# Mixer to output projection: sums, statistic, loads and units in another order around the last pairs

## What is computed

```python
uv = gelu(h @ w_in); u, v = split(uv, 2)            # w_in: 1024 x 4096
v = rmsnorm(v, v_norm_g)                            # over its 2048 channels
z = einsum("gts,bnsgc->bntgc", tril(w_s), v) + b_s  # within chunks of 128 tokens, 8 groups
x = x + g1 * ((u * z) @ w_out)                      # g1 is a modulation vector of c
```

## Time and profile before

| | |
|---|---|
| runs | 2631.08, 2641.82, 2637.97 us; median 2637.97 |
| the profiled execution | 2636.03 us, span 2634.0 us |
| granted TensorE clock, mean over the span | 0.987 of full speed |
| busy share of the span | TensorE 96%, DVE 60%, ACT 37%, POOL 6% |
| HBM traffic | 270.10 MB read, 88.08 MB written |

### The profile page before, as it was taken

One profiled execution on the slowest core, in us unless ns is written; L12 is line 12 of the kernel. 1 busy time (PEld: TensorE's weight loads), 2 busy tenths in 40 slices (PEclk: granted clock), 3 DMA queues, 4 the chain that ended last, 5 costly groups with the idle time before them and its releaser, 6 DMA issues.

```text
span 2634.0 us, 33661 instructions
## 1 busy us (share of the span) xinstructions
PE 2536.5 (96%) x12220; PEld 2069.6 (79%) x12220; DVE 1583.4 (60%) x1907; ACT 985.4 (37%) x1423; POOL 149.7 (6%) x151
## 2 busy tenths in 40 slices
PE   6999979999999999999999997999999999999999
PEld 4787767888788878888898886666688888888887
DVE  6777746667876756666632543777347656544442
ACT  4543333234544431111311232777426544421110
POOL 0000000000000000000000001666100000000000
PEclk9999989999999999999999998999999999999999
DMA  6244544322344475554132353465313332632311
GB/s 252 100 152 153 179 176 156 117 100 112 110 161 148 149 294 199 179 204 154 52 136 82 112 156 121 107 142 113 128 62 126 111 117 100 254 133 80 111 49 71
DMA packets 122981, 359.60 MB, mean 137 GB/s; under 512 B 12033, under 2 KB 28417, under 8 KB 118913
## 3 DMA queue, kind: packets, MB, share of 16 engines
q1 hardware_dynamic: 122880, 358.23, 40.5%
HBM read 270.10 MB, written 88.08 MB: 136 GB/s over the span
## 4 chain that ended last, share of the span: by engine, by line
PE 80%; DVE 9%; ACT 4%; DMA 3%; issue 3%; SPq 0%; DVEq 0%; ACTq 0%
PE PS L2024 23%; PE PS L2026 23%; PE PS L2025 22%; DVE KEEP L1944 2%; PE PS L2500 2%; PE PS L2487 2%; DMA MODRAW<-in_modw 1%; PE PS L2468 1%; PE PS L2128 1%; PE PS L2130 1%; PE PS L2129 1%; ACT PS L1262 1%; PE PS L2424 1%; PE PS L2469 1%; DMA RAW<-in_wt 1%
## 5 line engine op out<-in xcount | busy, mean ns | idle before, releaser
L2024 PE MATMUL PS<-HID_HI,W_HI 128*128 128x512 f32 x1024 | 400.3, 391 | 5.1 <-DVE HID_LO L1597 4.9
L2025 PE MATMUL PS<-HID_LO,W_HI 128*128 128x512 f32 x1024 | 398.8, 389 | 0.0
L2026 PE MATMUL PS<-HID_HI,W_LO 128*128 128x512 f32 x1024 | 398.8, 389 | 0.0
L374 ACT ACTIVATE W_HI<-RAW 128x1024 fp32r<-128x1024 f32 x114 | 119.5, 1059 | 614.1 <-PE PS L2026 509.8
L1443 DVE SCALAR_TENSOR_TENSOR X<-PS,MODV,X 128x1024 f32<-128x1024 f32 x124 | 159.1, 1283 | 300.4 <-PE PS L2026 291.7
L2024 PE MATMUL PS<-H_HI,W_HI 128*128 128x512 f32 x700 | 277.7, 397 | 3.9 <-DVE H_LO L1387 2.7
L2026 PE MATMUL PS<-H_HI,W_LO 128*128 128x512 f32 x700 | 273.8, 391 | 0.0
L2025 PE MATMUL PS<-H_LO,W_HI 128*128 128x512 f32 x700 | 273.5, 391 | 0.0
L2024 PEld LDWEIGHTS PS<-HID_HI,W_HI 128*128 128x128 f32 x1024 | 192.3, 188 | 48.6 <-DVE HID_LO L1597 7.9
L2026 PEld LDWEIGHTS PS<-HID_HI,W_LO 128*128 128x128 f32 x1024 | 192.3, 188 | 40.2
L2025 PEld LDWEIGHTS PS<-HID_LO,W_HI 128*128 128x128 f32 x1024 | 192.3, 188 | 39.6 <-issue 0.2
(11 more groups left out here) (223 smaller groups left out, 4947.5 us busy)
## 6 DMA issues: line engine op xcount, KB each, us to landing
RAW<-in_wt SPq DMA_DIRECT2D x208, 512.0 KB, 4.1
MODRAW<-in_modw SPq DMA_DIRECT2D x96, 512.0 KB, 3.4
HRAW<-hid_scratch SPq DMA_DIRECT2D x14, 2048.0 KB, 8.9
hid_scratch<-TN SPq DMA_DIRECT2D x90, 256.0 KB, 2.7
hid_scratch<-SCR SPq DMA_DIRECT2D x84, 256.0 KB, 3.2
x_scratch<-X SPq DMA_DIRECT2D x3, 4096.0 KB, 13.8
X<-x_scratch SPq DMA_DIRECT2D x6, 2048.0 KB, 8.4
QK<-qk_scratch SPq DMA_DIRECT2D x16, 768.0 KB, 6.3
```

Source lines behind the costliest of these rows:

```text
L374: act.activation(ring_view(W_HI, n), raw_view(n), ACT.Copy).then_inc(sem["w_hi"], 1)
L2024: pe.matmul(dst, w_hi, m_hi, start=first, stop=False)
L2025: pe.matmul(dst, w_hi, m_lo, start=False, stop=False)
L2026: return pe.matmul(dst, w_lo, m_hi, start=False, stop=last)
```

## The change

- **Late modulation rows.** In pairs 6 to 11 the third `mod_reduce` goes behind `c12` and `c21`.
- **The second pair of each stage.** `c11` of pair 1 goes ahead of the cuts and sums for pair 2 on DVE (mixer and both MLPs).
- **The statistic.** The column sums with their waits go from ahead of pair 12 to behind its product 2, the spread from behind product 2 to behind product 5, and `v_inverse` behind three cuts.
- **Loads.** SP fetches units 0 and 1 of v once product 6 of pair 12 is done, and WS_RAW after product 7; the wait on `v_kept` is gone. In pair 13 loads of v and u stand ahead of X, and two stores ahead of the second half of X.
- **Units.** ACT and DVE cut the third and fourth weight tiles of the projection behind the first two units. `v_scale(1)` and `v_scale(2)` trade places with `v_lo(0)` and others.
- **Gates.** `spatial(2)` goes into gate 0, `turn_z(2)` behind it, and `turn_v(3)` into gate 1.

```diff
 # SP
-                u_pair(Count(PAIRS - 2), 0)
-                p = Count(PAIRS - 1)
-                sp.wait_ge(sem["product"], PRODUCTS * (PAIRS - 1))
+                p = Count(PAIRS - 2)
+                store(p, 0, 0, 0, 0)
+                load_pair(p + 1)
+                sp.wait_ge(sem["product"], count_of(0, p, PRODUCTS, 6).v)
...
                 load_v(0)
-                sp.wait_ge(sem["v_kept"], 1)
+                load_v(1)
+                store(p, 2, 0, 1, 1)
+                sp.wait_ge(sem["product"], count_of(0, p, PRODUCTS, 7).v)
                 sp.dma_start(WS_RAW[:], spw).then_inc(sem["spw_in"], 16)
-                load_v(1)
+                store(p, 3, 1, 2, 0)
+                store(p, None, 1, 3, 1)
+
+                p = Count(PAIRS - 1)
                 sp.wait_ge(sem["product"], count_of(0, p, PRODUCTS, 2).v)
                 load_u(0)
+                sp.wait_ge(sem["hs_out0"], 64 * (PAIRS // 2))
+                load_v(2)
                 load_u(1)
                 load_raw(sp, Count(T_G + 2))
+                load_v(3)
+                store(p, 0, 0, 0, 0)
                 sp.dma_start(X[:, 0:4, :], xT[:, 0:4, :]).then_inc(sem["xm_lo"], 16)
-                store(p, 0, 0, 0, 0)
-                sp.wait_ge(sem["hs_out0"], 64 * (PAIRS // 2))
-                load_v(2)
-                load_v(3)
                 load_raw(sp, Count(T_G + 3))
                 store(p, 2, 0, 1, 1)
                 sp.wait_ge(sem["product"], count_of(0, p, PRODUCTS, 6).v)
                 load_u(2)
                 load_u(3)
+                store(p, 3, 1, 2, 0)
+                store(p, None, 1, 3, 1)
...
                 sp.dma_start(X[:, 4:8, :], xT[:, 4:8, :]).then_inc(sem["xm_hi"], 16)
-                store(p, 3, 1, 2, 0)
-                store(p, None, 1, 3, 1)
 # ACT, pair 13
                 finish(p, 1, 6, 1)
-                act.wait_ge(sem["product"], count_of(0, p, PRODUCTS, 6).v)
-                down_cut(UPS + 2)
                 z_keep(1)
                 finish(p, 1, 7, 2)
-                act.wait_ge(sem["product"], count_of(0, p, PRODUCTS, 7).v)
-                down_cut(UPS + 3)
                 v_hi(2)
                 uz_cut(1)
+                act.wait_ge(sem["product"], count_of(0, p, PRODUCTS, 7).v)
+                down_cut(UPS + 2)
+                down_cut(UPS + 3)
 # DVE, pair
+                    second = p.i is None and p.c == 1
+                    if second:
+                        c11(p, x)
                     block_cut(p + 1, 1 - x, A1)
                     weight_sums(p + 1, 1 - x)
...
-                    c11(p, x)
-                    if kind == "stat":
-                        v_inverse()
+                    if not second:
+                        c11(p, x)
...
                     block_cut(p + 1, 1 - x, S3)
+                    if kind == "stat":
+                        v_inverse()
                     c22(p, x)
...
-                    elif kind in ("u0", "u"):
-                        mod_reduce(dve, p * 3 - 2 * VPAIRS + 2)
                     c12(p, x)
                     c21(p, x)
+                    if kind in ("u0", "u"):
+                        mod_reduce(dve, p * 3 - 2 * VPAIRS + 2)
 # DVE, pair 13
                 v_scale(0)
                 cut_lo(dve, Count(T_G))
-                v_scale(1)
...
                 v_lo(0)
+                v_scale(1)
                 cut_lo(dve, Count(T_G + 1))
+                v_scale(2)
...
                 v_lo(1)
-                v_scale(2)
-                cut_lo(dve, Count(T_G + 2))
                 c21(p, 1)
                 uz_mul(1)
-                cut_lo(dve, Count(T_G + 3))
                 v_lo(2)
                 uz_cut(1)
+                cut_lo(dve, Count(T_G + 2))
+                cut_lo(dve, Count(T_G + 3))
 # TensorE
-                for v in range(4 * KT):
+                gate(0, lambda: spatial(2))
+                turn_z(2)
+                gate(1, lambda: turn_v(3))
+                for v in range(2, 4 * KT):
...
                 def statistic(n):
                     if n == 2:
+                        pe.wait_ge(sem["v_added"], 6 + 4 * VPAIRS)
+                        pe.wait_ge(sem["mod_red"], GMODS)
+                        # the 8 column sums, from V_TOT to V_COLS
...
+                    if n == 5:
                         pe.wait_ge(sem["v_diag"], 2)
...
-                pe.wait_ge(sem["v_added"], 6 + 4 * VPAIRS)
-                pe.wait_ge(sem["mod_red"], GMODS)
-                # the 8 column sums
                 pair(Count(PAIRS - 2), 0, False, statistic)
```

More of the change, by code:

```diff
@@ L2375, in statistic @@
                     if n == 2:
+                        pe.wait_ge(sem["v_added"], 6 + 4 * VPAIRS)
+                        pe.wait_ge(sem["mod_red"], GMODS)
+                        for half in range(2):
+                            for c in range(4):
+                                mm = pe.matmul(V_COLS[:, 4 * half + c:4 * half + c + 1],
+                                               V_TOT[:, half, c * P:(c + 1) * P], ONES[:, 0:1], start=True, stop=True)
+                        mm.then_inc(sem["v_col"], 1)
+                    if n == 5:
                         pe.wait_ge(sem["v_diag"], 2)
```

## The result

The changed kernel took 2610.07 us, median of four runs (2604.66 to 2611.83), against 2636.21 for the kernel before in runs on the same chip: ratio 0.9904, 95% interval 0.9892 to 0.9916. The profiled execution took 2611.83 us, with a span of 2609.8 at clock 0.99, 24.2 us less than that of before. The forecast was 2599 in a range of 2592 to 2612. So the sign and the range hold. The time is 11 us above the forecast, and the medians of the two kernels differ by 26.1 us, where 39.0 were forecast. The time is that of rival 1.

What follows compares the result with a forecast made beforehand. TensorE, busy 96% of the span, was taken as the bound, so only its waits and half-clock time could be won. Gains of 6.6 + 3.9 + 28.5 = 39.0 us gave 2599 us, range 2592 to 2612.

Steps and rivals of the forecast that it cites:

- rival 1: Waits move into pair 13, mask chain late: stretch to `spatial(3)` gives 19, rest 9; 2610 us, chance 0.25.
- late rows: Mixer pairs 7 to 11: `c21` no longer behind the third reduction, product 2 stops waiting; 6.6 us, bounds 4 and 6.6.
- pair 1, mixer: `c11` moves into DVE's idle time, product 6 stops waiting, pair 2's wait grows; net gain 1.4 us.
- pair 1, MLP 0: The wait ahead of product 6 and its slow stretch go, 3.55 us; about 1.0 comes back in pair 2; net 2.5.
- pair 12 to `spatial(3)`: 93.9 us before, 62.9 of bare work plus 2.5 of waits after; gain 28.5 us, bounds 19 and 31.0.
- comes at 4.5 to 5 us: Pairs 7 to 11: when the A1 cut comes after pair start, RAW being asked for at about that start.
- take the same bytes: SP's moved loads and stores around pairs 12 and 13 were costed at nothing.
- Rival 2: Pair 12's statistic keeps its wait, the whole old 5.6 us, with rival 1 too: 20 us gained, 2618, chance 0.03.
- The order of the DVE chain after spatial 0: DVE, about 24 us nearly unbroken until `v_lo(2)`, meets the spatials and turns with waits of at most 0.3 us.
- the column sums without idle time: In pair 12 TensorE reaches them at 8.2 us, reductions done; 4.6 us wait gone, sums take 1.8 us.
- the bare work of 62.9 us: Pair 12 to `spatial(3)` at full clock without waits: two pairs, two gates, sums, spread, three spatials, seven turns.
- The clock: Slower rival: transposes among matmuls keep the clock low from pair 12 on; 2655 us, chance 0.02.

Runs made afterwards that it cites:

- again: The changed kernel run once more unaltered: 2610.30 us, 0.9909 of the kernel before.
- hold_stores: Changed kernel, but in mixer pairs 6 to 11 SP holds the last three stores, and the third modulation row's load, until ACT's A1 cut: 2601.44 us, 0.9867.
- hold_mask: Changed kernel with those stores held and, in pair 12, loads ordered RAW tile, v unit 0, WS_RAW, other tile, v unit 1: 2595.93 us, 0.9855.
- loads_undone: Changed kernel with SP's order of loads and stores around pairs 12 and 13 as before: 2610.61 us, 0.9912.

## Why the prediction came out as it did

**The total was off by 11 us, the sign and range right.** That the time fell inside the range is in part luck: the range reached up to 2612 only to take in rival 1, and two terms of the forecast's own mechanism were missed. By terms, in the two profiles of the changed kernel:

| us gained | forecast | after | again |
|---|---|---|---|
| late rows | 6.6 | 2.2 | 4.2 |
| pair 1, mixer | 1.4 | 0.0 | 1.8 |
| pair 1, MLP 0 | 2.5 | 1.9 | 2.8 |
| pair 12 to `spatial(3)` | 28.5 | 19.0 | 19.0 |

**The step that failed** is one clause in the part on late rows: that A1 "comes at 4.5 to 5 us". I had RAW asked for at the start of the pair and landing as fast as a modulation row, 3.5 us. In the trace of before A1 already came 8.8 us into pair 9 on DVE; with held stores it comes at 7.9 to 8.7 in pairs 7 to 11, which the room still covers. In the changed kernel it came at 8.7, 10.3, 12.0 and 13.9 us in pairs 7 to 10. ACT's cut came 6.4 us after the issue where I followed it, because the edit itself brings the stores forward, and each late cut makes the next issue later. The next sentence even had the mechanism: "each microsecond would first eat 4 us of room ahead of product 2". The chain falls behind TensorE by about 1.7 to 2.5 us per pair, so the room is gone after two or three pairs. Then it also makes the diagonals of pair 12 late, which I had put at 13.5 to 15.4 us against TensorE's arrival at 18.1. Pair 12 took 27.1 and 25.2 us in the two profiles against 22.7 with held stores, so this costs 4.5 and 2.5 us there. `hold_stores` gives all of it back.

**The second failed step** is that SP's moved loads "take the same bytes" and cost nothing. Bytes are the same, but WS_RAW stands behind 1 MB of RAW, two units of v and a store, all issued within 3.1 us. Its landing took 9.2 us (10.0 in the second profile) and not the 6.9 of the earlier trace rows that I used as the upper end. I took 1.3 us of wait at spatial 0; it was 3.6 (4.0), with a lower clock behind it.

**Two sums don't add up.** The waits that I named behind pair 12 are 1.3 and twice 0.3 us, 1.9 and not 2.5; no row is behind the other 0.6. And the least gains of the terms (4, 2 and 19) give 2613, not the 2606 that I named as the upper end of my own range.

**Rival 1** gave the very number, 2610, with 19 us for the stretch. A part of the match is luck: it took 28 us off 2638, where 26.1 were gained on 2636.2, and its other terms were to give 9 us, where the two profiles show 4.1 and 8.8. Half of its mechanism is right: the mask's chain is late, and brings half clock. But of the 9.5 us missing in the stretch 5.0 lay in pair 12 in the first profile and 3.1 in the second, around the spread, which neither the forecast nor rival 1 had; and of rival 1's second wait behind spatial 0 only 0.3 us was seen. Rival 2, the statistic's wait, came true in small: 2.2 us of 5.6, not by ACT's tables alone but by late weights, behind whose cuts the root stands, as held stores alone take it away.

**What held.** The order of the DVE chain after spatial 0 (no wait on DVE in gates 0 to 2), the column sums without idle time, the bare work of 62.9 us to within 1 us (`hold_mask` takes 64.7 with 0.8 us of waits, so 63.9), and the price of the late rows, once free of the stores. Also the small size of pair 1: the net of 1.4 us, the wait moving on to pair 2, is what most profiles show. In the first profile of the changed kernel that moved wait was 1.79 us and a stretch at clock 0.66 followed it, which ate the gain:

```profile
135.10 0.50 PE L2033 MATMUL PS<-T_HI,WX_HI 128*128 128x512 f32 x1 [1.79 <-DVE TN L1583]
```

```profile
135.00:140.00 5.00, 4.90 (x14) 3.88 (x15) 1.83 (x4) 3.15 (x5) 0.00 (x0) 0.66 0.92 344
```

**The clock.** In `hold_mask` seven turns lie within 64.7 us among the matmuls, and the granted clock is 1.00 in each window. The Trainium skill ("TensorE: Matmul & The Clock Gate", Part 4: PE-mode transpose) says transposes don't count as busy for the clock in the way matmuls do; I drew from it that more such work between products would lower the clock, and the trace does not bear that out. By the 6.5 us reckoned for them the turns are about a tenth of this stretch, so it says nothing of longer streams of transposes. Where it was low in the windows read here, a wait stood ahead of it.

## What to carry to other kernels

An edit that makes work ready earlier also makes its stores leave earlier: look at what the queue is loading at that moment, and time the critical load with those stores beside it, not from the trace in which they came later. A wait hidden by room (4 us here) must be checked over several rounds: a round longer by 2 us spends it in two. When loads are moved forward, order them by who needs them first after the whole chain behind each (mask, two cuts), not by bytes.

## What the runs showed of the hardware

- A 512 KB load took from 3.5 us (MODRAW alone) over 5.0 and 6.9 (RAW, issued as two loads, without and with stores and a modulation row right behind it) to 9.2 (WS_RAW behind five transfers).
- POOL's mask of 128x1024 took 2.12 us in the kernel before and 2.11 in `loads_undone`, where a cut on DVE began at 360.02 and the mask at 360.08. It took 1.09 us in all the other twelve profiles; in the changed kernel DVE had ended at 362.12 and the mask began at 362.85. In the two with the long mask a cut on DVE had begun 0.05 and 0.06 us before the mask (377.44 and 360.02), and the mask ended 0.95 us after that cut's end, as if it had waited for it. That the one holds up the other fits; it wasn't tried by itself.
- A wait does not by its length alone tell whether the clock falls: it fell after 1.79 us in the first profile of the changed kernel and stayed at 1.00 after 2.50 us at the same place in `hold_mask`:

```profile
134.07 0.50 PE L2038 MATMUL PS<-T_HI,WX_HI 128*128 128x512 f32 x1 [2.50 <-DVE TN L1588]
```

```profile
134.00:139.00 5.00, 4.93 (x22) 4.08 (x23) 1.82 (x4) 3.14 (x5) 0.00 (x0) 1.00 0.90 347
```
